# Second attention of a two-block decoder: dilated scores as float32r on stacked halves, GpSimd preparing them, a fourth score bank, turns in the transpose banks

## What is computed

```python
h = rms_norm(x, norm_mix[l])
proj = h @ w_in[l]
o_a = nsa_mixer(...)            # 4 query heads: compressed, selected and window attention
o_b = dilated_mixer(...)        # 3 groups (window, stride) of 2 heads: (128,1) (512,4) (2048,16)
o_c = stick_breaking_mixer(...) # 6 heads
x = x + cat @ w_out[l]
h = rms_norm(x, norm_mlp[l])
x = x + jnp.square(jax.nn.relu(h @ w_up[l])) @ w_down[l]
```

## Time and profile before

| | |
|---|---|
| median of three runs | 1219.8 us |
| profiled execution | 1218.98 us |
| its span | 1217.2 us |
| TensorE busy | 95% of the span |
| VectorE, ScalarE, GpSimd busy | 52%, 35%, 40% |
| mean granted clock of TensorE | 0.949 |

### The profile page before, as it was taken

How to read it: one execution, slowest core, us unless ns; L and a number is a source line. 1 busy time by engine, 2 the same in 40 slices (tenths; PEclk the granted TensorE clock), 3 DMA queues, 4 the chain that set the end, 5 groups by cost and what they waited for, 6 DMA issues and landing times.

```text
span 1217.2 us, 16006 instructions
## 1 busy us (share of the span) xinstructions
PE 1153.3 (95%) x5777; PEld 978.9 (80%) x5777; DVE 628.0 (52%) x1121; ACT 423.6 (35%) x847; POOL 492.0 (40%) x489
## 2 busy tenths in 40 slices
PE   6999999999999999998989778999999999999998
PEld 5888888888788877897878767687878888888887
DVE  6869777685666727318436777433641231231321
ACT  5373587263365512223145665322130110110110
POOL 0000000000622419799970000003986776777772
PEclk9999999999999999999995897559999999999999
DMA  6322323323210103333330000001333232232321
GB/s 250 125 86 89 103 87 104 121 80 111 86 36 18 36 1 104 118 116 113 121 104 1 1 1 1 0 1 35 114 111 104 87 104 91 99 102 88 103 86 52
DMA packets 27277, 97.15 MB, mean 80 GB/s; under 512 B 3024, under 2 KB 3408, under 8 KB 27088
## 3 DMA queue, kind: packets, MB, share of 16 engines
q1 hardware_dynamic: 27216, 96.32, 23.9%
HBM read 94.21 MB, written 2.10 MB: 79 GB/s over the span
## 4 chain that ended last, share of the span: by engine, by line
PE 65%; issue 20%; DVE 9%; ACT 5%; POOL 1%; DMA 1%; SPq 0%; DVEq 0%; POOLq 0%; ACTq 0%
PE bank L1100 20%; PE bank L1102 20%; PE bank L1101 20%; PE bank L745 2%; PE bank L782 1%; PE bank L762 1%; DVE arena L1816 1%; DVE wl L1767 1%; ACT wh L1454 1%; DMA x<-x_in 1%; POOL wl L505 0%; DVE arena L2150 0%; DVE arena L1845 0%; ACT yh L1701 0%; DVE arena L2071 0%
## 5 line engine op out<-in xcount | busy, mean ns | idle before, releaser
L501 POOL TENSOR_TENSOR hold<-hold 128x2 f32<-128x2 f32 x117 | 29.0, 248 | 650.4 <-PE bank L1102 650.4
L1100 PE MATMUL bank<-xh,wh 128*128 128x512 f32 x568 | 226.5, 399 | 11.3 <-DVE xl L1736 9.6
L1102 PE MATMUL bank<-xh,wl 128*128 128x512 f32 x568 | 222.7, 392 | 0.0
L1101 PE MATMUL bank<-xl,wh 128*128 128x512 f32 x568 | 222.7, 392 | 0.0
L1100 PE MATMUL bank<-yh,wh 128*128 128x512 f32 x520 | 205.2, 395 | 8.2 <-POOL wl L505 4.9
L1101 PE MATMUL bank<-yl,wh 128*128 128x512 f32 x520 | 204.3, 393 | 0.0
L1102 PE MATMUL bank<-yh,wl 128*128 128x512 f32 x520 | 204.2, 393 | 0.0
L505 POOL TENSOR_TENSOR wl<-raw,wh 128x512 fp32r<-128x512 f32 x117 | 175.2, 1498 | 0.0
L504 POOL TENSOR_TENSOR wl<-raw,wh 128x512 fp32r<-128x512 f32 x117 | 156.6, 1339 | 9.8
L1100 PEld LDWEIGHTS bank<-xh,wh 128*128 128x128 f32 x568 | 107.5, 189 | 34.1 <-issue 10.9
L502 POOL TENSOR_SCALAR wh<-raw 128x1024 fp32r<-128x1024 f32 x117 | 126.3, 1080 | 0.0
(11 more groups left out here) (241 smaller groups left out, 1810.9 us busy)
## 6 DMA issues: line engine op xcount, KB each, us to landing
raw<-weight_units SPq DMA_DIRECT2D x173, 512.0 KB, 3.4
x<-x_in SPq DMA_DIRECT2D x4, 512.0 KB, 7.7
out_fm<-x SPq DMA_DIRECT2D x8, 256.0 KB, 2.0
arena<-tables SPq DMA_DIRECT2D x1, 1024.0 KB, 10.1
par<-params SPq DMA_DIRECT2D x1, 166.0 KB, 2.4
arena<-swa_table SPq DMA_DIRECT2D x1, 128.0 KB, 10.7
ident<-identity SPq DMA_DIRECT2D x1, 64.0 KB, 8.0
```

The lines of the kernel that those rows point to most:

```text
L501: pool.tensor_tensor(hold[:], hold[:], hold[:], ALU.add).then_inc(held, 1)
L1100: pe.matmul(out, lh, rh, start=start, stop=False)
L1101: pe.matmul(out, lh, rl, start=False, stop=False)
L1102: return pe.matmul(out, ll, rh, start=False, stop=stop)
```

## The change

1. Dilated scores are two float32r matmuls on 128 rows. For a query head the tile holds the high half in rows 0 to 63 and the low half in rows 64 to 127 (so it is doubled first, and rows 64 up are replaced by source less high). For a key head one tile holds the high half twice, another the low half twice. Score = stack x high keys + stack x low keys.
2. normalise is gone. GpSimd (pool_part) doubles and normalises one head at a time into 128 columns, TensorE turns it (12 turns at groups 17 to 44), ScalarE evicts it with the gain, in place, and GpSimd splits it into tiles of xh, xl, yh and yl that are free by then.
3. Strips take four score banks, 0, 1, 2 and 7.
4. The 12 turns and the six turns of finished pairs are counted as chunks in the transpose banks 3 and 4. VectorE's pair_out moves ahead of mask2 and frees the bank.
5. Order ahead of the attention: F2 and kc go before G3; the compressed keys' turn follows G3; then F5 and F3. The weight units are loaded in that order. Of F6's two VectorE steps each comes one round earlier.
6. Three output tiles are begun inside the attention, not four.

The core of the diff (GpSimd's block also moves behind make_attention, its splits unchanged, with pool_part called after the split of unit U_OUT2 + 3):

```diff
-ITEMS2 = {-1: ("kcT", 0, 1), 22: ("dT", 0, 1), 24: ("dT", 1, 1), 26: ("dT", 2, 1), 28: ("dT", 3, 1), 30: ("dT", 4, 1),
-          32: ("dT", 5, 1)}
+TURNS2 = {17: ("q", 0), 19: ("q", 1), 21: ("q", 2), 23: ("q", 3), 25: ("q", 4), 27: ("q", 5), 29: ("k", 0), 31: ("k", 1),
+          33: ("k", 2), 35: ("k", 4), 40: ("k", 5), 44: ("k", 3)}
-TAIL = {-1: (0,), 0: (1,), 1: (2,), TURN_LAG - 1: (3,)}
-BEGUN = 4
+TAILS = {1: {-1: (0,), 0: (1,), 1: (2,), TURN_LAG - 1: (3,)}, 2: {-1: (0,), 0: (1,), 1: (2,)}}
+BEGUN = {1: 4, 2: 3}
-SCORE_BANKS = {1: (0, 1, 2), 2: (0, 1, 2)}
+SCORE_BANKS = {1: (0, 1, 2), 2: (0, 1, 2, 7)}
...
-    seg2 += [("nT", j, "D") for j in range(6)] + [("hT", 0, "A")] + [("G3", t, "A") for t in range(4)]
-    seg2 += [("F", 2, "D"), ("F", 5, "D"), ("F", 3, "D"), ("kc", 0, "A")]
+    seg2 += [("nT", j, "D") for j in range(6)] + [("hT", 0, "A"), ("F", 2, "D"), ("kc", 0, "A")]
+    seg2 += [("G3", t, "A") for t in range(4)] + [("kcT", 0, "A"), ("F", 5, "D"), ("F", 3, "D")]
...
                 if kind == "dil":
-                    return [(dq[rows, n, k * P:(k + 1) * P], dk[rows, n + 1 - w // P:n + 1, k * P:(k + 1) * P])]
+                    m = 2 * k + h
+                    return [(dil_tile("q", m, 0)[:, qs], dil_tile("k", m, low)[:, (n + 1) * P - w:(n + 1) * P]) for low in range(2)]
...
+                def turn_chunk(key, src):
+                    c = chunk_of[key]
+                    pe.wait_ge(*chunk_taken(c - 2))
+                    for t in range(TB):
+                        mm = pe.transpose(B[3 + c % 2][:, t * P:(t + 1) * P], src[:, t, :], ident[:])
+                    mm.then_inc(s["pt_ready"], 1)
...
+                    if a == 2 and i in TURNS2:
+                        k = DIL_ORDER.index(TURNS2[i])
+                        pe.wait_ge(dil_doubled, k + 1)
+                        turn_chunk(TURNS2[i], doubles[k % 2])
...
+            def pool_part(pool):
+                def double(k):
+                    name, m = DIL_ORDER[k]
+                    if k == 0:
+                        pool.wait_ge(heads_split, len(F_ORDER))
+                    if k == 1:
+                        last_cmp = [g for g in groups if batches[g["b"]]["kind"] == "cmp"][-1]["strip0"]
+                        pool.wait_ge(*strip_read(last_cmp))
+                    if k >= 2:
+                        pool.wait_ge(dil_split, k - 1)
...
+                    pool.tensor_tensor(doubles[k % 2].rearrange("p t (c d) -> p t c d", c=2),
+                                       raw_[:, :, m * HD:(m + 1) * HD].unsqueeze(2).to_broadcast([P, TB, 2, HD]),
+                                       rq.unsqueeze(3).to_broadcast([P, TB, 2, HD]), ALU.mult).then_inc(dil_doubled, 1)
+
+                def split_dil(k):
+                    name, m = DIL_ORDER[k]
+                    src = doubles[k % 2].rearrange("p t q -> p (t q)")
+                    pool.wait_ge(*chunk_taken(chunk_of[name, m]))
+                    pool.tensor_scalar(dil_tile(name, m, 0), src, 1.0, 1.0, ALU.mult, ALU.mult).then_inc(dil_high, 1)
+                    pool.wait_ge(dil_high, k + 1)
+                    rows = slice(HD, P) if name == "q" else slice(0, P)
+                    pool.tensor_tensor(dil_tile(name, m, name == "k")[rows, :], src[rows, :], dil_tile(name, m, 0)[rows, :],
+                                       ALU.subtract).then_inc(dil_split, 1)
+
+                for k in range(len(DIL_ORDER) + 1):
+                    if k < len(DIL_ORDER):
+                        double(k)
+                    if k > 0:
+                        split_dil(k - 1)
```

More of the change, by code:

```diff
@@ L259, in attention_two, with with_chunks @@
     return batches, groups + dilated
-def with_chunks(groups, batches, per_chunk):
+def with_chunks(groups, batches, per_chunk, extra=None):
     strip = chunk = 0
-    for g in groups:
+    taken = {}
+    for i, g in enumerate(groups):
         g["strip0"] = strip
@@ L274, in with_chunks @@
         chunk += len(g["chunks"])
-    return groups
+        for key in (extra or {}).get(i, ()):
+            taken[key] = chunk
+            chunk += 1
+    for i in sorted(i for i in extra or {} if i >= len(groups)):
+        for key in extra[i]:
+            taken[key] = chunk
+            chunk += 1
+    return taken
 def two_block_kernel(nc, x_d, weights_d, params_d, tables_d, swa_d, ident_d, out_d):
@@ L656, in probs_ready, with chunk_ready, chunk_taken, pair_turned @@
                 return (s["sprobs"], k + 1) if is_stick(i) else (s["probs"], i - k + 1)
+            extra = {}
+            if a == 2:
+                for p, end in enumerate(pairs):
+                    extra.setdefault(end + TURN_LAG, []).append(("pair", p))
+                for i, key in TURNS2.items():
+                    extra.setdefault(i, []).append(key)
+            chunk_of = with_chunks(groups, batches, 2 if a == 1 else 4, extra)
+            def chunk_ready(c):
+                return s["pt_ready"], c + 1
+            def chunk_taken(c):
+                return s[("pt_even", "pt_odd")[c % 2]], c // 2 + 1
+            def pair_turned(p):
+                return (s["pairT"], p + 1) if a == 1 else chunk_ready(chunk_of["pair", p])
             before7, last7 = {}, None
@@ L790, in pair_turn @@
                             pe.wait_ge(*fin_of(b))
-                    if before7[("pair", p)]:
+                    if a == 1 and before7[("pair", p)]:
                         pe.wait_ge(*before7[("pair", p)])
+                    if a == 2:
+                        turn_chunk(("pair", p), otok[:, slot[p]])
+                        return
                     for t in range(TB):
@@ L902, in pt_copy @@
                 eng.wait_ge(s["pt_ready"], c + 1)
-                if c >= slots:
-                    eng.wait_ge(s["o_done"], last_of_chunk[c - slots] + 1)
+                earlier = [k for k in range(c - slots, -1, -slots) if k in last_of_chunk]
+                if earlier:
+                    eng.wait_ge(s["o_done"], last_of_chunk[earlier[0]] + 1)
                 n = len(blocks) * P
@@ L1347, in _ @@
             turn_hidden()
[L1348 to L1350 removed]
+            f_tile(2)
             pe.wait_ge(evac_a, FREE[("hT", 0)][1])
@@ L2121, in _ @@
                               v4[0:31, 1, 0:1], None, ALU.mult).then_inc(heads_normed, 1)
+            for j in (5, 3):
+                scale_f(j)
+                low_f(j)
             def item(key):
```

254 lines of the change are left out of this document (124 added, 130 removed).

## The result

Four runs of the kernel after took 1206.82 to 1210.32 us, median 1208.62; four of the kernel before, on the same chip, 1217.84 to 1220.04, median 1218.99. The ratio is 0.9914, 95% interval [0.9894, 0.9934]: faster by 10.4 us, where 30.8 were forecast, and 1.6 us above the upper end of the range. The profiled execution took 1210.32 us (span 1208.1). Of the runs further on, four are left out of medians and ratios as slow: 1863 us of the kernel before, 4301 us in e9, 6243 us in e14, and 1203.93 us in e15, which lies so near the others that e15's ratio is less sure than its interval says (about 0.982 with it).

What follows compares the result with a forecast made beforehand. TensorE, busy 1153.3 of 1217.2 us, was taken as the bound, alone in the dilated groups, with engines waiting on each other in the middle. Savings 18 + 3.6 + 1 + 1.5 + 6 + 0.7 = 30.8 us gave 1189; range 1170 to 1207.

Steps and rivals of the forecast that it cites:

- The stretch before: Ahead of the attention, F2 covers G3's wait for bank 3: 3.6 us saved, and 1 us of slow restart.
- The start of the attention: First compressed scores no longer wait for strip 3's reader, with four banks: 1.5 us saved, between 0 and 5.4.
- The middle: Stick, selected and window groups, 664 to 760 us: 6 us saved in all, ends 18 saved and 8 lost.
- the bank's gain: In the middle, a fourth score bank lets TensorE issue ahead during VectorE's stick read: 12 us saved.
- signs of being right: Shorter dilated scores, clock there above 0.53, no TensorE wait before 571, stick wait below 8 us, GpSimd about 37 us.
- signs of being wrong: VectorE's scans and small instructions growing over 4 us, TensorE waiting for doubling, dilated stage at 0.5 throughout, stick wait unchanged.
- The turns: In the middle, six more turns and their use of transpose banks cost 1 and 1 us, the port 4.
- The port: In the middle, GpSimd's hold on the port shared with VectorE: 4 us lost, 12 at most, 0 at least.
- rival D: Slower: GpSimd's doubling comes late in the turns and TensorE waits in order; 1227 at 3.2 us per turn. Chance 0.06.
- The dilated stage: Eight dilated groups, 760 to 818 us: shorter float32r scores and a higher clock save 18 us, between 12.3 and 26.
- B's condition: Rival B: clock stays at 1.2 GHz under the dilated groups, port takes the middle's gain; 19 us saved, 1201. Chance 0.30.
- The end: After the last turn, tile 3 covers GpSimd's split of unit 4: 0.7 us saved, -1 to 2.4.

Runs made afterwards that it cites:

- e9: Kernel after with ScalarE's copy ahead of the second softmax step and GpSimd's doubling as TENSOR_SCALAR: 1200.14 us, 0.9864 of the kernel before.
- e14: Kernel after with ScalarE's and VectorE's copies early and ScalarE's evictions of turns ahead of its first softmax steps: 1197.56 us, 0.9852 of the kernel before.
- e15: e9 with the split's subtraction also a TENSOR_SCALAR, so low parts hold full values (no kernel to use): 1195.39 us, 0.9806 of the kernel before.
- e2: Kernel after with three score banks, turns still in the transpose banks: 1205.36 us, 0.9898 of the kernel before.
- e5: The kernel after run again, unchanged: 1205.06 us, 0.9888 of the kernel before.
- e10: e6 with three score banks in place of four: 1205.28 us, 0.9915 of the kernel before.
- e6: Kernel after with ScalarE's copy of transposes ahead of the second softmax step: 1197.95 us, 0.9848 of the kernel before.
- e11: e6 without the twelve new doublings, turns, evictions and splits (no kernel to use): 1183.89 us, 0.9716 of the kernel before.
- e8: Kernel after without the twelve new doublings, turns, evictions and splits (no kernel to use): 1197.17 us, 0.9820 of the kernel before.
- e18: e6 run again, unchanged: 1200.56 us, 0.9855 of the kernel before.
- e7: Kernel after with GpSimd's doubling as four TENSOR_SCALAR in place of one TENSOR_TENSOR: 1203.85 us, 0.9870 of the kernel before.
- e12: Kernel before with only ScalarE's copy moved ahead of the second softmax step: 1214.91 us, 0.9972 of the kernel before.
- e13: e6 with VectorE's copy also ahead of the scan of group i + 2: 1203.60 us, 0.9892 of the kernel before.
- e4: Kernel before with only the dilated scores as two float32r matmuls of 128 rows, from wrong tiles (no kernel to use): 1198.97 us, 0.9830 of the kernel before.

## Why the prediction was wrong

**The stretch before: right.** 4.6 us forecast (3.6 and 1). The first stick scores come at 602.26 us, not 607.08, while the turns ahead of G3 came 0.6 us later, so 5.4. The wait at G3 is gone; F2 starts behind the turns at full clock:

```profile
567.90 0.30 PE L1434 MATMUL bank<-ident,arena 31*128 31x31 f32 x2
568.13 0.50 PE L1199 MATMUL bank<-xh,wh 128*128 128x512 f32 x1
```

**The start of the attention and the stick groups up to 21: a gain, larger than forecast.** 1.5 us forecast (0 to 5.4), 4.75 gained, with no turns yet. The wait for a strip's reader was replaced by one of 2.12 us for soft2 and one of 2.64 us for ScalarE's late copy:

```profile
631.81 0.90 PE L748 MATMUL bank<-ident,arena 128*128 128x128 f32 x3 [2.12 <-ACT arena L870]
635.35 1.11 PE L768 MATMUL bank<-arena 128*128 128x64 f32 x4 [2.64 <-ACT arena L875]
```

**The middle: wrong, and this is the step that failed.** The forecast put the bank's gain at 12 us ("VectorE finds them ready"), took 1 us for turns in one of two transpose banks and said of the values only that TensorE "still stops" at them. I had listed who waits for VectorE's read of a strip, but not what stands in ScalarE's queue behind the step that waits for it. The next late thing was a copy of 0.3 us with nothing to wait for of its own, behind soft2. With it behind soft2 the fourth bank gains nothing that can be measured (e2 against e5); with it ahead, some 7 us (e10 against e6) with turns, and the middle is 8.4 us shorter than before without them (e11). Of the 20.4 us that the forecast was off, this term is 12; 2 are the turns and 1.6 the end, next, and the rest is of the size of the spread (the kernel after itself stood at 0.9914 and, in e5, at 0.9888, where its median of 1205.06 us lies inside the forecast's range; the gain, 14 us there, is still less than half of what was forecast). The two traces put the whole miss here: from group 21 to the dilated groups 14.5 us were lost where 6 saved were forecast. But a trace tells this stretch only within some 7 us, as the last section shows. The forecast's signs of being right all came out, the stick wait below 8 us among them, while the time did not: I had named the wait that would go, and no row for the one that would take its place. One of its signs of being wrong came out too, VectorE's scans and small instructions growing by more than 4 us in sum (6.2, below).

**The turns: undersized.** 1, 1 and 4 us were taken, the 4 for the port. e5 against e8 says 8 us for all three, with the copy early 14 to 17 (e11 against e6 and e18). My reading, which no run tests by itself, is that a stretch that waits less shows more of what is put into it.

**The port: the mechanism right, the size in time not settled.** GpSimd did 35 us between 640 and 750, no instruction of TensorE waited for its doubling (rival D did not come about), and VectorE paid. Groups of VectorE's instructions, 664 to 760 us (count, busy, mean ns of one), after and then e8, where GpSimd is silent:

```profile
L991 DVE TENSOR_TENSOR_SCAN arena<-ones,arena 128x384 f32<-128x384 f32 (+3 forms) x14 | 13.3, 953 | 0.5
L1051 DVE TENSOR_TENSOR arena<-arena 128x256 f32<-128x256 f32 x6 | 4.0, 661 | 0.2
L1043 DVE TENSOR_TENSOR den<-den,gates 128x4 f32<-128x4 f32 x6 | 2.8, 474 | 0.2
L1039 DVE TENSOR_SCALAR den<-rsum 128x4 f32<-128x4 f32 x6 | 2.7, 448 | 0.2
```

```profile
L988 DVE TENSOR_TENSOR_SCAN arena<-ones,arena 128x384 f32<-128x384 f32 (+3 forms) x14 | 12.1, 862 | 0.5
L1048 DVE TENSOR_TENSOR arena<-arena 128x256 f32<-128x256 f32 x7 | 3.0, 425 | 0.2
L1036 DVE TENSOR_SCALAR den<-rsum 128x4 f32<-128x4 f32 x7 | 1.2, 167 | 0.2
L1040 DVE TENSOR_TENSOR den<-den,gates 128x4 f32<-128x4 f32 x7 | 1.2, 166 | 0.2
```

(953 - 862) x 14, (661 - 425) x 6, (474 - 166) x 6 and (448 - 167) x 6 are 1.3 + 1.4 + 1.8 + 1.7 = 6.2 us of VectorE, half of the 12 that were the upper end. The scans are of the same shapes in both, and VectorE's copies out of a bank did not grow (512 columns: 690 ns in both). The same four groups are 3.5 us longer than in e8 when the doubling is a TENSOR_SCALAR (e7), and 1.0 us when the split's subtraction is one too (e15): VectorE's loss goes with GpSimd's TENSOR_TENSOR. What it costs in time is not told apart: 2 us from e5 to e7 and 5 to 7 from e9 to e15 are each open by 5 or 6, and 4 were taken. The pair at 703.0 and 703.2 us above is the mechanism itself. The Trainium skill, SBUF — State Buffer, "Who interferes with whom", says that the shared pair of ports is an exclusive lock and that the one that comes second waits for the whole instruction; that pair agrees with it. The 12 us that I had set beside that rule, an estimate from a count of some 30 instructions, were twice what VectorE lost.

**The dilated stage: right within what can be told.** 18 us forecast. The first trace shows 14.9. Over it and the seventeen profiles of the experiments with the new scores (all but e12) the stage takes 38.7 to 48.7 us, mean 44.1: 18.8 less than the 62.9 before. But 62.9 is one trace; in e12, whose dilated scores are also the old ones, the stage took 57.0 us, and against that the mean gain is 12.9. B's condition, half clock throughout, did not hold in one of them; in the kernel after it held from 795 to 811 us (the rows are in the last section).

**The end: no gain seen.** 0.7 us forecast. From the last turn (825.05 us) to tile 4 (835.38) are 10.3 us, counted from the turn's start, against 9.2 before. The 1.9 us of idling came as forecast, but TensorE ran at half clock behind it (0.57 in 828 to 832 us), and that I had not priced. Over all profiles tile 0 to the end takes 393.0 to 398.4 us, so a difference of 0.9 has no sign that can be told:

```profile
825.05 0.60 PE L790 MATMUL bank<-ident,arena 128*128 128x128 f32 x4
...
827.53 0.47 PE L1199 MATMUL bank<-yh,wh 128*128 128x512 f32 x1 [1.88 <-DVE yl L1074]
```

**The sum again**, from the table of distances: gained 4.9 ahead of group 5, 4.75 up to group 21 and 14.9 in the dilated stage; lost 14.5 from group 21 to the dilated groups and 0.9 behind tile 0. That is 9.15, and the spans differ by 9.1 (1217.2 and 1208.1).

## What to carry to other kernels

When a wait is removed, list every engine's queue from the point that it frees, and look for a short instruction that is ready but stands behind one that is not: here a copy of 0.3 us behind a softmax step cost 13 us where no dilated turns were in the way (e8 against e11), and 2 to 3 in the kernel before. Move what another engine waits for ahead of what itself waits, on an engine with slack; on VectorE, which had little, it gained nothing (e13). And measure the part that pays, alone, before the parts that prepare it: the new scores by themselves gave 20 us, the whole change 10.

## What the runs showed of the hardware that was not expected

**The clock in the dilated stage rose, and differs from trace to trace.** Before, TensorE was busy 55.6 of 58 us at 0.53. In the kernel after, at different moments of the stage:

```profile
764.00:784.00 20.00, 15.14 (x100) 13.26 (x100) 16.23 (x56) 10.02 (x36) 0.00 (x0) 0.91 0.00 1
784.00:795.00 11.00, 9.55 (x60) 8.75 (x60) 6.09 (x20) 4.37 (x15) 0.00 (x0) 0.81 0.00 0
795.00:811.00 16.00, 15.28 (x74) 14.54 (x72) 4.59 (x9) 3.82 (x10) 0.00 (x0) 0.50 0.01 2
```

In the first 20 us it had 2.4 GHz about four fifths of the time (a mean of 0.91 between the levels 0.5 and 1) with TensorE idle for a quarter of it; in the last 16 it had 1.2 GHz while TensorE was nearly always busy. Ahead of that fall TensorE had stood for a copy of ScalarE's:

```profile
792.44 0.44 PE L748 MATMUL bank<-ident,arena 128*128 128x128 f32 x2 [1.45 <-ACT arena L875]
```

In e14 the stage kept 0.96 and took 38.7 us. From its first scores to tile 0, with nearly the same instructions on TensorE each time, it took 40.8 us at 0.92 (e5), 42.7 at 0.84 (e4), 45.0 at 0.81 (e6), 48.0 at 0.75 (the kernel after) and 48.7 at 0.72 (e18): the lower the clock, the longer the stage, by up to 10 us. With the old scores it is 57.0 at 0.64 (e12) and 62.9 at 0.57. What decides between these is not settled by the runs.

**The same instructions took 7 us more at a lower clock.** e4 differs from the kernel before only in the dilated scores, and yet it took 134.0 us from group 5 to the dilated groups, not 126.7, at a clock of 0.77 in 664 to 760 us in place of 0.88. e6 and e18, one kernel, took 131.9 and 126.3 us, at 0.78 and 0.86 from group 5 to the dilated groups. So one profile against one profile does not tell 7 us of this stretch apart; the ratios of four to twelve runs each, with an unchanged copy of the kernel (e5, e18) beside them, tell about five.
